# Eight blocks of an input projection: computed for the first 128 tokens in front, for the other 192 inside a later loop

## What is computed

```python
z = rmsnorm(h, g_norm) @ w_in                  # 2048 x 5656 columns
q, kv, gt, cv = jnp.split(z, SPLITS, axis=-1)  # 1024, 1536, 24, 3 x 1024
q = rmsnorm(q.reshape(b, L, N_HEADS, HEAD_DIM), qk_gain[0])
b_gate, c_gate, hc = jnp.split(cv, 3, axis=-1)
u = c_gate * hc
conv = b_gate * (y + bias)                     # y: causal convolution of u over 3 tokens, by channel
attn = nsa_prompt(...) or nsa_attend(...)      # compressed, selected and window keys, 8 heads
h = x + concat(rmsnorm(attn), rmsnorm(conv)) @ w_out
qh = rmsnorm(h) @ wq                           # experts: best 16 of 16384 for each of 8 heads
act = gelu(einsum("td,trkd->trk", n, u_tab[eidx]))
h = h + einsum("trk,trkd->td", g * act, v_tab[eidx])
y = h + sigmoid(rmsnorm(h) @ w_gate) * (p @ w_ple)
```

## Time and profile before

| | us |
|---|---|
| median of 3 runs | 2659.68 |
| lowest and highest | 2645.7, 2661.2 |
| the profiled execution | 2654.51 |
| its span, first to last instruction | 2652.7 |

### The profile page before, as it was taken

The page is one execution under the profiler, slowest core; times in us unless marked ns, Lnnn a source line. Parts: engine busy times, 40 slices in busy tenths (PEclk is TensorE's granted clock), DMA queues, the critical chain, the costliest instruction groups (busy, mean ns, idle before and its releaser), DMA issues.

```text
span 2652.7 us, 20815 instructions
## 1 busy us (share of the span) xinstructions
PE 1878.3 (71%) x8059; PEld 910.2 (34%) x8059; DVE 1153.9 (43%) x2082; ACT 335.1 (13%) x672; POOL 972.5 (37%) x644
## 2 busy tenths in 40 slices
PE   7999999989936668778789644444544534578788
PEld 3444445763912236423257311111111111222224
DVE  1000042231066753654452466566565675644442
ACT  1000002230012322110010110101001012000002
POOL 0000000000045643542352356666566665645540
PEclk9999998969967776689889776776767777799889
DMA  7463234526569998999899999999999999999996
GB/s 252 122 203 127 97 120 136 180 96 239 174 278 414 421 400 319 347 413 379 344 416 385 376 418 421 421 421 421 421 421 422 419 422 417 388 416 415 417 419 231
DMA packets 207430, 871.89 MB, mean 329 GB/s; under 512 B 24935, under 2 KB 49383, under 8 KB 123530
## 3 DMA queue, kind: packets, MB, share of 16 engines
q0 software_dynamic: 92160, 671.13, 61.4%
q1 hardware_dynamic: 115034, 198.74, 21.8%
q10 hardware_dynamic: 144, 0.79, 0.1%
HBM read 858.59 MB, written 12.95 MB: 329 GB/s over the span
## 4 chain that ended last, share of the span: by engine, by line
PE 52%; DMA 34%; POOL 4%; issue 4%; DVE 4%; ACT 2%; SPq 0%; DVEq 0%; PEldq 0%; ACTq 0%; POOLq 0%
DMA arena<-in_peer_v,arena 23%; PE bank L1821 15%; PE bank L1462 12%; DMA arena<-in_peer_u,arena 3%; POOL arena L600 3%; PE bank L1467 3%; DMA arena<-in_w_out 2%; PE bank L1512 2%; PE bank L1640 2%; DMA arena<-in_peer_wq 2%; PE bank L1616 2%; PE bank L1772 2%; PE bank L1876 2%; DMA arena<-in_state_win 2%; PE bank L1752 1%
## 5 line engine op out<-in xcount | busy, mean ns | idle before, releaser
L1821 PE MATMUL bank<-arena 128*32 128x512 f32 x2560 | 644.6, 714 | 614.9 <-DMA arena<-in_peer_v,arena 538.6
L1333 DVE CUSTOM_DVE_ANT_0 arena<-arena 128x2048 f32<-128x2048 f32 x320 | 732.1, 2292 | 641.3 <-DMA arena<-in_peer_u,arena 637.9
L600 POOL DMA_INDIRECT arena<-in_peer_v,arena x320 | 516.5, 1614 | 737.9 <-PE bank L1821 677.0
L595 POOL DMA_INDIRECT arena<-in_peer_u,arena x320 | 455.8, 1424 | 867.2 <-DVEq L1312 759.6
L1821 PEld LDWEIGHTS bank<-arena 128*32 128x32 f32 x2560 | 169.9, 129 | 1066.9 <-issue 993.7
L1462 PE MATMUL bank<-arena 128*128 128x512 f32 (+2 forms) x800 | 326.3, 567 | 7.0 <-PE bank L1467 5.7
L1462 PEld LDWEIGHTS bank<-arena 128*128 128x128 f32 (+1 forms) x800 | 147.4, 198 | 176.6 <-issue 176.5
L884 ACT ACTIVATE arena<-arena 128x4 f32<-128x4 f32 x80 | 16.4, 205 | 916.0 <-DVE arena L1333 915.8
L1876 PE MATMUL bank<-arena 128*128 128x512 f32 x256 | 112.7, 596 | 0.0
L1005 DVE TENSOR_TENSOR arena<-arena 128x1024 f32<-128x1024 f32 (+1 forms) x3 | 3.5, 1218 | 211.7 <-ACT arena L636 211.7
L1772 PE MATMUL bank<-arena 128*128 128x192 f32 x512 | 88.9, 337 | 9.3 <-DMA arena<-in_peer_wq 9.3
(11 more groups left out here) (201 smaller groups left out, 1550.1 us busy)
## 6 DMA issues: line engine op xcount, KB each, us to landing
arena<-in_w_in SPq DMA_DIRECT2D x22, 2048.0 KB, 7.9
arena<-in_w_out SPq DMA_DIRECT2D x8, 2048.0 KB, 8.7
arena<-in_peer_wq SPq DMA_DIRECT2D x8, 2048.0 KB, 8.1
arena<-in_w_out SPq DMA_DIRECT2D x16, 1024.0 KB
arena<-in_peer_wq SPq DMA_DIRECT2D x16, 1024.0 KB
arena<-in_ple_gate SPq DMA_DIRECT2D x32, 512.0 KB, 16.3
arena<-in_ple_gate SPq DMA_DIRECT2D x6, 2048.0 KB, 11.6
arena<-in_cache_kv SPq DMA_DIRECT2D x64, 128.0 KB, 2.5
```

The source lines that it names most:

```text
L595: pool.indirect_dma_start(u_row[j], None, I["peer_u"][0], bass.IndirectOffsetOnAxis(idx[:, i, c + j:c + j + 1], 0)).then_inc(u_in[j], 16)
L600: pool.indirect_dma_start(v_row[j], None, I["peer_v"][0], bass.IndirectOffsetOnAxis(idx[:, i, c + j:c + j + 1], 0)).then_inc(v_in[j], 16)
L1333: dve.tensor_tensor_reduce(out=u_row[j], in0=u_row[j], in1=rep_of(i), scale=1.0, scalar=0.0, op0=ALU.mult, op1=ALU.add, accum_out=a4[:, pa ...
L1821: ins = pe.matmul(bank[q][32 * j:32 * j + 32, :], diag[:, k % 2, j, :], v_row[j][:, 512 * q:512 * q + 512], start=(s == 0), stop=(s == SST ...
```

## The change

Blocks 0 to 7 are computed in front for tile 0 alone. For the other 192 rows (tile 1 and the samples) they are computed once more, channel-major, between the value products of steps 0 to 6 of the loop, from weights that are loaded a second time in quarters (`ring_c`, three slots). For this the normalized and turned input of the 192 rows goes to DRAM (`xn_dram`) and comes back later. The convolution of tile 0 stays by tokens; that of the 192 rows is made by channels in DVE's `late_conv`, their head norms by sums of squares that PE makes. Items 0 to 15 move to steps 8 to 15, two a step. The value products of all steps go to four column groups of one bank, alternating between two banks by group of tokens; the four tiles add up in PSUM, each v buffer is given back by itself, and the reduction L1830 and the wait for `h_seen` go. The diff, cut:

On SP:

```diff
         sp.wait_ge(u_ready, 1)
-        sp.dma_start(O[4][0, 0], cu[126:128, 1, :]).then_inc(u_out, 16)
-        for w in range(2):
-            sp.dma_start(O[7][0][:, w, :], cu[NT - 2 + w:64:NT, 2, :]).then_inc(u_out, 16)
         for d, dst in ((1, sh1), (2, sh2)):
-            for t in range(3):
-                sp.dma_start(dst[d:ROWS[t], t, :], cu[0:ROWS[t] - d, t, :]).then_inc(shift_a, 16)
-            sp.dma_start(dst[0:d, 1, :], cu[128 - d:128, 0, :]).then_inc(shift_a, 16)
+            sp.dma_start(dst[d:128, 0, :], cu[0:128 - d, 0, :]).then_inc(shift_a, 16)
...
+        sp.wait_ge(xn_ready, 1)
+        for a in range(2):
+            sp.dma_start(xn_dram[:, 1536 * a:1536 * a + 1536], xn_half[a].rearrange("p c t -> p (c t)")).then_inc(xn_out, 16)
...
+        def fill_c(f):
+
+            blk, q = divmod(f, 4)
+            if f >= 3:
+                sp.wait_ge(rc_used, f - 2)
+            c0 = LATE_COLS[blk]
+            sp.dma_start(ring_c[f % 3], w_view["in"][:, 4 * q:4 * q + 4, c0:c0 + 512]).then_inc(rc_in[f % 3], 16)
+
+        sp.wait_ge(xn_out, 32)
+        sp.wait_ge(mm_done, N_WQ + 1)
+        sp.dma_start(xn_T.rearrange("p c t -> p (c t)"), xn_dram).then_inc(xnT_in, 16)
+        fill_c(0)
+        fill_c(1)
+        sp.wait_ge(mm_done, N_WQ + 4)
+        for f in range(2, 32):
+            fill_c(f)
...
-        sp.wait_ge(mm_done, N_WQ + 4)
+        sp.wait_ge(rc_used, 32)
         key_load(0)
         key_load(1)
         value_load(0)
```

New helpers and what runs in which step:

```diff
+    LATE = [("q", 0), ("q", 1), ("b", 0), ("c", 0), ("h", 0), ("b", 1), ("c", 1), ("h", 1)]
+    LATE_COLS = [512 * j + {"q": 0, "b": QKV + GATES, "c": QKV + GATES + CONV, "h": QKV + GATES + 2 * CONV}[kind]
+                 for kind, j in LATE]
+
+    def items_of(k):
+
+        if k < 8:
+            return ()
+        return (2 * (k - 8), 2 * (k - 8) + 1) if k < 16 else (k,)
+
+    def by_sample(ap, n):
+
+        return ap.rearrange("p (b t) -> p b t", b=NB)[:, :, 0:n]
```

On POOL and ACT:

```diff
             for j in range(4):
                 if k:
-                    pool.wait_ge(v_used, 4 * (k - 1) + 2 * (j // 2) + 2)
+                    pool.wait_ge(v_used, 4 * (k - 1) + j + 1)
...
         def acc_out(i):
 
-            act.wait_ge(peer_mm, i + 1)
+            act.wait_ge(v_used, 4 * SSTEP * (i + 1))
             if i:
-                act.wait_ge(red_mm, i)
-            if i < 3:
-                act.wait_ge(rep_act, i + 1)
-                act.wait_ge(rep_dve, i + 1)
+                act.wait_ge(h_seen, i)
+            if i == 3:
+                act.wait_ge(rep_act, 3)
+                act.wait_ge(rep_dve, 3)
+            r = tile_of(i)[1]
             for q in range(4):
-                ins = act.activation(acc[:, 512 * q:512 * q + 512], bank[q][:, :], ACT.Copy)
...
+        def late_out(b):
+
+            kind, j = LATE[b]
+            if kind == "h":
+                return
+            act.wait_ge(rc_used, 4 * b + 4)
+            if kind == "q" and j:
+                act.wait_ge(sums_mm, 1)
+            if kind == "c":
+                act.wait_ge(sums_mm, 2)
...
+            for s in range(4):
+                src_P, src_S, c = bank[4 + s][:, 0:128], bank[4 + s][:, 128:192], 4 * j + s
+                if kind == "q":
...
+                    ins = act.activation(sq_q[:, s, :], bank[4 + s][:, 0:192], ACT.Square)
+                elif kind == "b":
+                    act.activation(conv_P(c), src_P, ACT.Copy)
+                    ins = act.activation(conv_S(c), src_S, ACT.Copy)
+                else:
+                    act.activation(u_ext[:, s, 2:130], src_P, ACT.Copy)
+                    ins = act.activation(by_sample(u_ext[:, s, 130:210], NT + 2)[:, :, 2:NT + 2], by_sample(src_S, NT), ACT.Copy)
+            ins.then_inc(cz_ev, 1)
...
+        def late_behind(k):
+
+            if k == 1:
+                root(stats[:, 212:228], stats[:, 228:244])
+            if k == 4:
+                u_rows_out(0)
+            if k < 7:
+                late_out(k + 1)
+            if k == 6:
+                act.wait_ge(cv_done, 2)
+                for c in range(8):
+                    act.activation(sq_c[:, c, 0:128], conv_P(c), ACT.Square)
+                    ins = act.activation(sq_c[:, c, 128:192], conv_S(c), ACT.Square)
+                ins.then_inc(sqc_ready, 1)
...
-            if k < EARLY:
-                before_gelu(k)
+            items = items_of(k) if k < EARLY else ()
+            if items:
+                before_gelu(items[0])
...
+            if k < 8:
+                late_behind(k)
+            for v in items[1:]:
+                before_gelu(v)
```

On DVE (`late_conv` in part; `head_norm`, `scale_heads`, `conv_norm`, `scale_conv` are some ten small operations each):

```diff
+        def late_conv(j):
+
+            if j:
+                dve.wait_ge(ut_mm, 1)
+            dve.wait_ge(chan_in, 16 * 6)
+            dve.wait_ge(cz_ev, 4 if j == 0 else 6)
...
+            dve.wait_ge(rc_used, 20 if j == 0 else 32)
+            for x in range(4):
+                for u, src in ((u_ext[:, x, 2:130], bank[4 + x][:, 0:128]),
+                               (by_sample(u_ext[:, x, 130:210], NT + 2)[:, :, 2:NT + 2], by_sample(bank[4 + x][:, 128:192], NT))):
+                    ins = dve.tensor_tensor(u, src, u, ALU.mult)
+            step(ins)
+            dve.sem_inc(ch_ev, 1)
```

```diff
+        late = {1: head_norm, 2: lambda: scale_heads(0), 3: lambda: (scale_heads(1), late_conv(0)),
+                6: lambda: late_conv(1), 7: conv_norm, 8: scale_conv}
```

On PE:

```diff
+        blocks(0, 8, 1)
+        blocks(8, 2, 2)
+        pe.wait_ge(n1_ready, 1)
+        pe.wait_ge(u_ready, 1)
+        pe.wait_ge(chan_in, 16 * 6)
+        for c in range(8):
+            pe.transpose(bank[6][:, 32 * c:32 * c + 32], cu[96:128, 0, 128 * c:128 * c + 128], ident[96:128, 96:128])
+            pe.transpose(bank[7][:, 256 + 16 * c:272 + 16 * c], state_rows[0:16, 128 * c:128 * c + 128], ident[0:16, 0:16])
+        root_rows(bank[7], 0, 4, 5).then_inc(hist_mm, 1)
         for n in (10, 11):
-            product(None, n + 1, 16 * (n // 2) + 16, n % 2, GATES if n == 10 else 512)
+            product(n + 1, 16 * (n // 2) + 16, n % 2, 3 if n == 10 else 2, GATES if n == 10 else 512)
             pe.wait_ge(w_used, 4 + 2 * (n + 1))
             pe.sem_inc(mm_done, 1)
+        pe.wait_ge(hist_ev, 1)
...
         def weighted_rows(k):
 
             i, s = divmod(k, SSTEP)
-            if s == 0 and i:
-                pe.wait_ge(h_seen, i)
+            if s == 0 and i >= 2:
+                pe.wait_ge(acc_ev, i - 1)
             pe.wait_ge(diag_ready, k + 1)
-            for j0 in (0, 2):
-                for j in (j0, j0 + 1):
...
-            if s == SSTEP - 1:
-                pe.wait_ge(v_used, 4 * k + 4)
...
+            for j in range(4):
+                weighted_tile(k, j)
+
+        def weighted_tile(k, j):
+
+            i, s = divmod(k, SSTEP)
+            pe.wait_ge(v_in[j], 16 * (k + 1))
+            for q in range(4):
+                ins = pe.matmul(bank[i % 2][32 * q:32 * q + 32, :], diag[:, k % 2, j, :], v_row[j][:, 512 * q:512 * q + 512],
+                                start=(s == 0 and j == 0), stop=(s == SSTEP - 1 and j == 3))
+            ins.then_inc(v_used, 1)
+
+        def late_quarter(b, q):
+
+            f = 4 * b + q
...
+            pe.wait_ge(rc_in[f % 3], 16 * (f // 3 + 1))
+            for x in range(4):
+                for k in range(4):
+                    ins = pe.matmul(bank[4 + x][:, 0:192], ring_c[f % 3][:, k, 128 * x:128 * x + 128], xn_T[:, 4 * q + k, :],
+                                    start=(q == 0 and k == 0), stop=(q == 3 and k == 3))
+            ins.then_inc(rc_used, 1)
...
+        for q in range(4):
+            late_quarter(0, q)
         for k in range(EARLY):
-            item(k)
+            if k in late:
+                late[k]()
+            if k < 7:
+                for j in range(4):
+                    late_quarter(k + 1, j)
+                    if j == 0:
+                        pe.wait_ge(diag_ready, k + 1)
+                    weighted_tile(k, j)
+                continue
+            if k == 8:
+                pe.wait_ge(roots_set, 2)
+                root_rows(bank[2], 0, 246, 247).then_inc(roots_mm, 1)
+            for v in items_of(k):
+                item(v)
             weighted_rows(k)
```

More of the change, by code:

```diff
@@ L631, in z_out @@
             act.wait_ge(mm_done, wait)
+            if wait <= 8:
+                act.activation(dst(0, slice(0, 512)), bank[3 * (n % 2)][:, :], ACT.Copy, scale=stats[:, 3:4]).then_inc(mm_ev, 1)
+                return
             for t in range(2):
@@ new lines, in u_rows_out @@
+        def u_rows_out(j):
+            act.wait_ge(ut_mm, j + 1)
+            if j:
+                act.wait_ge(u_out, 48)
+            act.activation(u_rows[0:82, :], bank[3][0:82, :], ACT.Copy).then_inc(ut_ev, 1)
+            act.wait_ge(ut_ev, j + 1)
+            cols = slice(512 * j, 512 * j + 512)
+            act.dma_start(O[4][0, 0][:, cols], u_rows[0:2, :]).then_inc(u_out, 16)
+            for w in range(2):
```

(33 more changed lines are left out.)

260 lines of the change are left out of this document (178 added, 82 removed).

## The result

| | before | after |
|---|---|---|
| median of 20 runs | 2655.72 us | 2670.73 us |
| the profiled execution's span | 2652.7 us | 2672.9 us |
| mean granted clock of PE | 0.823 | 0.768 |
| through the DMA engines | 871.89 MB | 907.12 MB |

The ratio is 1.0059 with a 95% interval of 1.0043 to 1.0075. The kernel is 0.6% slower, where 1.6% faster was forecast. The time lies in the range; the sign is wrong. Of the prediction's cases it is the one of no change beyond 1%, which it gave 0.28.

The account below looks back on a forecast made before the run. PE was taken to bound the input projection, DMA transfers at 422 GB/s the loop's steady steps. Front -131, loop steps 0 to 15 +127 and value products -34 gave -38 us: 2616.5, forecast as 2618 us, range 2562 to 2684.

Parts of the forecast that it names:

- no change beyond 1%: Whole kernel: the time stays within 1% (26.6 us) of the kernel before; chance 0.28.
- front and stage behind, up to step 0: Input blocks 0 to 7 for one tile, and the stage behind: -131 us in the prediction.
- steps 0 to 15 of the loop: Expert loop with late blocks and paired items: from 367 to 494 us, +127 us in the prediction.
- value products and all behind step 15: Value products over four column groups without the reduction, counted where PE leads and at the end: -34 us.
- The size of the wait: Front: PE waits for the ninth half's weights, late behind the window-state copy; 32 us charged.
- A step is bound by DMA: 33 us: Loop steps with late weight quarters: 12.6 MB of transfers set the step at 33 us, not PE's 26.4.
- the step before needed no gather for the next one and takes 28: Loop steps 3 and 6, before the long ones: no gather needed for the next step, 28 us each.
- It counts where PE leads: Shorter value products gain at step 16 (-8), steps 17 to 20 and 23 to 26 (-10), and step 24's boundary (-9 us).
- rival D: Value products: the four column groups don't run together, products stay at 5.4 us; 2633 us, chance 0.47 together with the forecast case.
- A: Front: the window-state copy doesn't hold the weight loads, so the wait falls away; 2585 us, chance 0.18.
- C: Late steps: weight quarters starve behind gathers, steps average over 40 us; at 46 the kernel takes 2696 us; chance 0.15.
- B: Steps 8 to 15: items 8 to 15 take 190 us, pairs at steps 8 to 11 take 25 each; 2656 us, chance 0.20.

Follow-up runs that it names:

- run 1: Changed kernel with the 4 MB copy of the window state issued behind block 9's weight loads instead of block 3's: 2654.07 us, ratio 0.9981.
- run 2: Changed kernel with the window-state copy and the bias table (its write and 17 loads) moved behind the loads of blocks 9 and 11: 2647.95 us, ratio 0.9959.
- Runs 3 to 5: Kernel before with only the new value products (2656.55 us); with 28 of 32 weight-quarter loads of project_b and queries_b left out (2604.80 us); with both (2578.53 us).
- run 7: Changed kernel loading only the first three quarters of the late blocks' weights and multiplying all 32 from them: 2640.20 us, ratio 0.9922.
- run 9: Changed kernel with VectorE's dot products before its h-block wait, diagonals before the convolution, sums of squares behind step 7's value products: 2661.61 us, ratio 1.0004.
- run 6: Kernel before with only items 0 to 15 moved into steps 8 to 15, two a step: 2683.89 us, ratio 1.0092.
- run 11: Changed kernel with copy and table later, dot products first, and five small loads of taps and gains moved from SP's queue to POOL's: 2626.99 us, ratio 0.9891.
- run 12: Kernel before with the window-state copy issued behind the loads of block 8 instead of block 3: 2669.85 us, ratio 1.0054.

## Why the prediction was wrong

Its terms, between the same marks (the first value product of step 0, the end of those of step 15):

| term | forecast | measured |
|---|---|---|
| front and stage behind, up to step 0 | -129 | -129.7 (771.4 to 641.6) |
| steps 0 to 15 of the loop | +125 | +147.6 (367.1 to 514.7) |
| value products and all behind step 15 | -34 | +2.3 |
| sum | -38 | +20.2 |

*The front* was right, in its parts too. The early blocks end at 186.8 (forecast 187), with one gap, and compression starts 131.8 us sooner. The size of the wait was right (32.4 against 32) and its attribution half wrong: 18 of it went with the copy and the other 14 with the bias table (runs 1 and 2). The 60 us from the copy's issue to the landing, from which the 32 were worked out, were taken behind both writes, so the sum came out right under too narrow a name.

```profile
126.46 8.87 PE L1660 MATMUL bank<-arena 128*128 128x512 f32 x15 [32.40 <-DMA arena<-in_w_in]
```

*Steps 0 to 15* cost 23 us more than forecast, nearly all of it in the late steps, and it was a matter of size. By the ends of their value products steps 0 to 6 took 237.8 us, forecast 214; step 7 23.4 (26), steps 8 to 11 87 (90), steps 12 to 15 166.5 (162). "A step is bound by DMA: 33 us" comes near for steps 1, 2 and 5 (37.0, 32.7, 30.6). What failed is "the step before needed no gather for the next one and takes 28": steps 3 and 6 took 34.0 and 31.6, since the gathers run ahead of VectorE all the same and share the transfers with the quarters (DMA share 0.98 and 0.88 in the windows of after). In step 3 (739.9 to 773.9) POOL issues four u and four v gathers as in any other step; VectorE takes up the u rows of these only 40 us later, so it is in step 4 that the next u gathers come late. The first two of the four u gathers, and VectorE's first dot product with these rows:

```profile
741.42 0.94 POOL L658 DMA_INDIRECT arena<-in_peer_u,arena  x1 [0.30 <-issue]
742.66 0.94 POOL L658 DMA_INDIRECT arena<-in_peer_u,arena  x1 [0.30 <-issue]
...
784.38 2.29 DVE L1457 CUSTOM_DVE_ANT_0 arena<-arena 128x2048 f32<-128x2048 f32 x1
```

Step 0 took 28.6, not 22, at 413 GB/s: its bytes, too, filled the transfers. The forecast of 41 for step 4 was good (43.3).

*The value products* are the step that failed by kind, with 36 of the 58 us. I wrote "It counts where PE leads: step 16, -8; steps 17 to 20 and 23 to 26, -10; the boundary at step 24, -9". Four groups do run side by side, 3.64 us for 16 products in steps 17 to 26 against 5.38, so rival D falls. But "where PE leads" was read from stages in which PE is busy 0.85 and 0.82 of the time at a DMA share of 0.95 and 0.98. The prediction even contradicts itself: from the same query steps it took that "a step is bound by DMA: 33 us, not 26.4". Six of the eight steps with weights (17 to 20, 24 and 26) have a wait of 4.0 to 5.4 us for their last quarter, which stood in PE's timeline of before and which I didn't use:

```profile
1187.95 6.67 PE L1752 MATMUL bank<-arena 128*128 128x512 f32 x8 [5.07 <-DMA arena<-in_w_out]
```

With that wait there, the transfers and not PE end the step, and most of the time taken from PE goes into a longer wait. Runs 3 to 5 show it from both sides: 3 us with the loads, 26 us without. In after the waits are 30.5 us in project_b (20.6 before) and 23.3 in the queries (9.3). The chain of after names the quarters at three of these steps:

```profile
1206.73 30.80 DMA arena<-in_w_out
1390.19 36.80 DMA arena<-in_peer_wq
1458.78 32.46 DMA arena<-in_peer_wq
```

By stretches: from step 15's last product to project_b -6.7 us (forecast -8, right), project_b and the steps up to the queries +4.8, the queries up to the first value product of step 26 +6.9, all behind it -2.7.

*The rivals.* A (no hold in front) and C (starving quarters; median to landing 14.6 us, steps 1 to 6 at 34.9 us on average, not over 40) didn't happen. Of B nothing came either: pairs at 8 to 11 took 87 us and the sample steps 166.5, against its 100 and 190. By the rule of the Trainium skill (DMA: Bandwidth & Descriptors, Queues, rings and completion order) I had estimated 12.5 us a quarter; the page of the profile of after has 14.6 in the median. The 50 us a step that were worked out from it didn't come.

*The change as a whole.* It loads 33.6 MB more and moves some 170 us of PE from a stretch that PE bound into one that transfers bound already. The 113 us up to gelu 7 are 34 for the bytes (run 7), some 38 for VectorE's two long steps (48.0 and 42.0 in run 7, where the others take 26.2), of which another order gave 15 back (run 9), and the other 41 for steps of 26.2 us even without the bytes, where gathers alone make 20. That these 41 are PE's own 26 us is worked out by subtraction; no run took both bytes and products away. Of the next 31, 22 appear in run 6 too, where only the items move; that they come from fewer gathers beside the sample chain is argued and not shown, and the other 9 are open.

## What to carry to other kernels

Before you call a stretch bound by PE, look at what PE waits for in it: here it was busy 0.9 of the query steps and yet waited 4 to 5 us for a transfer in every second of them, and the time taken from PE there came back as waiting. A trial kernel without the loads tells the two cases apart. When an engine in front gets faster, list everything else on the queue that feeds it (copies, tables, loads in small elements), since the old pace may have covered them one after the other: here three came to light, each when the one before was moved, and moving the third was worth under 1 us in front. And work that is moved under a transfer-bound loop costs its bytes, its place in the other engines' program order, and the cover that the loop gave to someone else.

## What was new about the hardware

- Three loads of taps (in_conv_w), 1024 elements of 4 bytes each, took 9.2 us of SP's queue in the changed kernel, 35.6 behind the copy (run 2: 27.9 of them in one piece of the chain), and 2.9 on POOL's queue (run 11).
- A load of a few rows (in_state_conv) took 41.9 us to land right behind the 4 MB copy (run 11), and issues of other transfers behind it on SP's queue lasted 50.4 instead of 32.4 us (run 12).
- The steady steps got a slower PE and didn't notice. In before PE is busy 73 of 160 us at a granted clock of 0.72, in after 50 at 0.62. The first two value tiles of a step, after 12.4 us of waiting, run at the lower of the two levels (1.2 GHz, a granted clock of 0.50 in their 3.7 us), the last one at the upper (1.00); a step lasts 20 us either way. Timeline of PE in after:

```profile
1791.94 3.74 PE L2035 MATMUL bank<-arena 128*32 128x512 f32 x16 [12.39 <-DVE arena L1466]
1796.23 1.20 PE L2035 MATMUL bank<-arena 128*32 128x512 f32 x8 [0.55 <-DMA arena<-in_peer_v,arena]
1798.70 1.06 PE L2035 MATMUL bank<-arena 128*32 128x512 f32 x8 [1.27 <-DMA arena<-in_peer_v,arena]
```
